# One product in each up quarter of a feed-forward made as two narrower ones, at widths that change from quarter to quarter

## The chip, the cores and the metric

The kernel runs on one core of one Trainium2 chip. The metric is the device time of one execution in microseconds (us). A smaller number is better. The time before is the median of 3 runs.

## What is computed

Two transformer blocks, one after the other, on 256 tokens of 1024 features in fp32. The part that the change touches is the feed-forward of the first block:

```
h = rmsnorm(x, ffn_norm[i])
u = causal_dwconv(h @ w_up[i], conv_w[i], conv_b[i])
x = x + (jax.nn.gelu(u) * (h @ w_gate[i])) @ w_down[i]
```

`w_up` and `w_gate` are 1024 x 2816, `w_down` is 2816 x 1024. Ahead of it stand the attention and the retention of the first block, behind it a gated embedding, and then the second block: a delta rule, sparse attention and a mixture of 16 experts.

## The kernel before

Every fp32 product is made as three products of the type fp32r. A weight matrix `w` is split into a high part `w_hi` and a rest `w_lo`, and so are the activations (`h_hi`, `h_lo`); the sum of high x high, high x low and low x high is added up in one place of PSUM. The function `three` issues these three. In the up projections `weight_stationary` is true: a 128 x 128 piece of the weights is the stationary operand, and 256 columns of `h`, one for each token, are the moving operand. Its passes are `((0, 0), (0, 1), (1, 0))`: pass 0 is `w_hi` with `h_hi`, pass 1 is `w_hi` again with `h_lo`, pass 2 is `w_lo` with `h_hi`. In a row of the profile the moving operand is named first (`h_lo,w_hi`).

The weights come as a stream of quarters of 128 x 1024, which pass through a ring of six slots (`raw`, `w_hi`, `w_lo`). SyncE issues the loads, ScalarE copies the high part (L635), GpSimd subtracts for the low part (L594, two instructions of 128 x 512 for a quarter), and TensorE waits for `lo_done` at the head of each quarter.

`feature_quarter` multiplies one quarter: a loop over 8 values of `k`, and `three` in each, so 24 products of 256 columns that all add into the same half bank (`dst`, 128 x 256). `up_block` makes four such quarters: two of `w_up` and then two of `w_gate`. `ffn_step` makes two up blocks and a down block of four quarters with 512 moving columns (`row_quarter`, 12 products in each). The step is written out once as the start, then runs four times in a loop (`Fori(1, FFN_STEPS)`, with `FFN_STEPS` = 5), and a last up block stands behind the loop, followed by the products of the gated embedding (`p_hi`, `p_lo`) and the last down products. In the start, the first two quarters are made by `first_quarters`, which does not call `feature_quarter`; `spread_root` puts in a small product of its own.

The order of TensorE's work is the order in which the program writes it.

Once the first two quarters of an up block are there, VectorE scales them (L2334), ScalarE and VectorE do the convolution (L763, L2342), ScalarE applies the gelu (L775), VectorE multiplies by the gate (L2348, L2351), and the result is split again for the down products (ScalarE L780, VectorE L2354).

Of the kernel before, what the change touches and what calls it, by code (L numbers as in the profile page):

```python
# [29 lines left out]
S = 256  # L30
NT = S // P
D = 1024
KD = D // P
# [24 lines left out]
B_FFN_LAST = B_FFN + 3 * FFN_STEPS  # L58
# [255 lines left out]
def program(nc, weights, smalls, x_in, p_in, vec_in, rows, con_in, slot_in, sel_in, pos_in, out):  # L314

    ctx = ExitStack()
    with ctx:
        made = {}

        def sem(name):  # L320

            if name not in made:
                made[name] = ctx.enter_context(nc.semaphore(name))
            return made[name]

        def sb(name, cols, dt=F32):
            return ctx.enter_context(nc.sbuf_tensor(name, [P, cols], dt))
# [7 lines left out]
        h_hi = sb("h_hi", KD * S, F32R)  # L335
        h_lo = sb("h_lo", KD * S, F32R)
# [8 lines left out]
        h_hi, h_lo, g_hi, g_lo = (x[:, :].rearrange("p (k s) -> p k s", s=S) for x in (h_hi, h_lo, g_hi, g_lo))  # L345
# [47 lines left out]
        bias = bias.rearrange("p (h s) -> p h s", s=S)  # L393

        (conv, act, ple, _, norm_row) = carve(1536, 2 * 512, 2 * 512, NT * D, NT * 512, D)
        conv = conv.rearrange("p (b f s) -> p b f s", b=2, s=S)
        act = act.rearrange("p (b n) -> p b n", b=2)
# [39 lines left out]
        for of, at, name in ((g_upper, 0, "g_upper_first"), (g_tri, 4 * PLE_CHUNKS * S, "g_tri_first")):  # L437
# [3 lines left out]
        (o_squares,) = carve(ATTENTION, 1024)  # L441

        (_, _, _, _, e_act, selectors, comb, comb_t, route, slot_con, slot_route, logit_rows) = carve(0, TILES * D, TILES * D, NT * SLOTS, TILES * S, 1024, DENSE * P, NT * N_EXPERTS, S, 354, SLOT_CON_N,
                          200, S)

# [86 lines left out]
        def pair(u):  # L532

            return bank[2 * (u % 2)], bank[2 * (u % 2) + 1]
# [621 lines left out]
        def _(pe):  # L1156
            mm = nc.tensor.matmul

            def three(dst, w, h, start, stop, weight_stationary):

                passes = ((0, 0), (0, 1), (1, 0)) if weight_stationary else ((0, 0), (1, 0), (0, 1))
                for n, (i, j) in enumerate(passes):
                    a, b = (w[i], h[j]) if weight_stationary else (h[j], w[i])
                    ins = mm(dst, a, b, start=start and n == 0, stop=stop and n == 2, skip_group_check=True)  # L1164
                return ins

            def quarter(q):
                return w_hi[:, ring(q)], w_lo[:, ring(q)]

            def await_quarter(n):  # L1170

                pe.wait_ge(sem("lo_done"), n + 1)
# [7 lines left out]

                pe.wait_ge(sem(f"pair_free{u % 2}"), 2 * (u // 2) + 2)

            def feature_quarter(n, q, dst, h=(h_hi, h_lo), norm=None, middle=None):


                if isinstance(n, int) and n == 0:
                    pe.wait_ge(sem("first_low_half"), 1)
                else:
                    await_quarter(n)
                w = [x.rearrange("p (k c) -> p k c", c=P) for x in quarter(q)]  # L1190
                for k in range(KD):
                    if isinstance(n, int) and n == 0 and k == KD // 2:
                        await_quarter(n)
                    if middle and k == KD // 2:
                        middle()
                    if norm is not None:

                        pe.wait_ge(sem("h_lo_done"), KD * norm + k + 1)
                    ins = three(dst, [x[:, k, :] for x in w], [x[:, k, :] for x in h], k == 0, k == KD - 1, True)
                ins.then_inc(sem("quarter_done"), 1)  # L1200

            def feature_project(b, u, beside=lambda f: None, norm=None, middle=lambda f: None, bank_free=lambda i: None):
# [30 lines left out]
            def token_half(q, u, f, t):  # L1233

                if t == 0:
                    await_quarter(q)
                w = [x.rearrange("p (k c) -> p k c", c=512) for x in quarter(q)]
                for j in range(2):
                    k = 2 * f + j
                    ins = three(pair(u)[t][:, :], [x[:, j, :] for x in w],  # L1240
                                [x[:, k, t * P:(t + 1) * P] for x in (h_hi, h_lo)], k == 0, k == KD - 1, False)
                if t:
                    ins.then_inc(sem("quarter_done"), 1)
                return ins
# [22 lines left out]
            def spread_root(n, to):  # L1267

                i = ROOT_ROWS.index(n)
                pe.wait_ge(sem("root_widened"), NT * i + NT)  # L1270
                for t in range(NT):
                    ins = mm(bank[to][:, t * P:(t + 1) * P], root_wide[:, t, :], ident, start=True, stop=True)
                ins.then_inc(sem("root_spread"), 1)
# [163 lines left out]
            def first_quarters(q0, norm, of):  # L1437

                dst = [of[:, f * S:(f + 1) * S] for f in range(2)]
                await_quarter(q0)  # L1440
                half_quarter(q0, q0, dst[0], range(4), norm)
                await_read(8)
                turn_half(norm, 1)
                await_quarter(q0 + 1)
                half_quarter(q0 + 1, q0 + 1, dst[1], range(4), norm, first_of_bank=False)
                for f in range(2):
                    half_quarter(q0 + f, q0 + f, dst[f], range(4, KD), norm).then_inc(sem("quarter_done"), 1)

            def up_block(base, q0, i, free, norm=None):

                pe.wait_ge(sem(f"pair_free{1 - i}"), free)
                if norm is not None:
                    first_quarters(base + q0, norm, pair(1 - i)[0])
                for f in range(0 if norm is None else 2, 4):
                    if norm is not None and f == 3:
                        spread_root(norm, 4)
                    feature_quarter(base + q0 + f, q0 + f, pair(1 - i)[f // 2][:, f % 2 * S:(f % 2 + 1) * S])

            def down_block(base, q0, n_up, start, stop, count=4):
                for k in range(count):  # L1460
                    if k % 2 == 0:

                        pe.wait_ge(sem("act_lo_done"), n_up + k // 2 + 1)
                    row_quarter(base + q0 + k, q0 + k, bank[4:8], (g_hi, g_lo), k, start and k == 0,
                                stop and k == count - 1)


            def ffn_step(base, n, start):
                up_block(base, 0, 0, n + 8, 1 if start else None)
                up_block(base, 4, 1, n + 10)  # L1470
                if start:
                    pe.wait_ge(sem("root_row_ready"), 2)
                down_block(base, 8, n, start, False)

            ffn_step(4 * B_FFN, 0, True)
            with pe.Fori(1, FFN_STEPS) as i:
                ffn_step(i * 12 + 4 * B_FFN, i * 2, False)
            n = 2 * FFN_STEPS
            up_block(4 * B_FFN_LAST, 0, 0, n + 8)

            pe.wait_ge(sem("pair_free0"), n + 10)
            pe.wait_ge(sem("p_split"), 2)
            q = 4 * B_PLE_DOWN
            for t in range(NT):
                if t == 1:
                    pe.wait_ge(sem("act_lo_done"), n + 1)
                for k in range(2):
                    await_quarter(q + k)
                    for c in range(2):
                        ins = three(bank[2 * t + c][:, :], [x[:, c * 512:(c + 1) * 512] for x in quarter(q + k)],  # L1490
                                    [x[:, k, t * P:(t + 1) * P] for x in (p_hi, p_lo)], k == 0, k == 1, False)
# [3 lines left out]
            for c in range(2):  # L1495
                for k in range(2):
                    await_quarter(q + 2 + k)
                    for t in range(NT):
                        ins = three(bank[4 + 2 * t + c][:, :], [x[:, c * 512:(c + 1) * 512] for x in quarter(q + 2 + k)],
                                    [x[:, k, t * P:(t + 1) * P] for x in (g_hi, g_lo)], False, k == 1, False)  # L1500
# [16 lines left out]
            for t in range(NT):  # L1517
                for f in range(4):
                    ins = token_half(4 * (B_PLE_GATE + 1) + f, 23, f, t)
# [324 lines left out]
            for i in range(2):  # L1844
                for f in range(4):
                    q = 4 * (B_PROJ + i) + f
# [10 lines left out]
                    w = [x.rearrange("p (f k c) -> p f k c", f=2, c=P) for x in quarter(q)]  # L1857
                    for j in range(2):
                        if j:
                            delta_slot(2 * (q - 4 * B_IQ) + 1, delta_step)  # L1860
                        for k in range(4):
                            ins = three(pair(u)[f % 2][:, j * S:(j + 1) * S], [x[:, j, k, :] for x in w],
                                        [x[:, 4 * (1 - i) + k, :] for x in (g_hi, g_lo)], k == 0, k == 3, True)
# [85 lines left out]
            for t in range(NT):  # L1949
                ins = nc.tensor.transpose(bank[3][0:N_EXPERTS, t * P:(t + 1) * P], comb[:, t, :], ident)  # L1950
# [4 lines left out]
            for e in range(DENSE):  # L1955
                ins = mm(bank[2][:, e * S:(e + 1) * S], selectors[0:N_EXPERTS, e * P:(e + 1) * P], comb_t, start=True, stop=True)
# [21 lines left out]
            for k in range(4):  # L1978
                if k % 2 == 0:
                    pe.wait_ge(sem("expert_lo_done"), k // 2 + 1)  # L1980
                q = 4 * (B_MOE + 2) + k
# [10 lines left out]
            def y_banks(tile):  # L1992
                return bank[4 + 2 * (tile % 2)], bank[5 + 2 * (tile % 2)]
# [74 lines left out]
            for c in range(2):  # L2068
                for k in range(2):
                    ins = three(y_banks(GROUPS)[c][:, :], [x[:, c * 512:(c + 1) * 512] for x in quarter(N_QUARTERS + last + k)],  # L2070
                                [x[:, k, 0:P] for x in (g_hi, g_lo)], False, k == 1, False)
# [1052 lines left out]
```

## Time and profile before

| | |
|---|---|
| median of 3 runs | 842.63 us (842.61 to 843.84) |
| the profiled execution's own time | 846.45 us |
| its span, first to last instruction | 844.6 us |
| mean granted TensorE clock | 0.991 |
| TensorE matmul busy | 823.0 us, 97% |
| TensorE weight load busy | 737.5 us, 87% |
| VectorE, ScalarE, GpSimd busy | 59%, 55%, 56% |

A matmul record's end is modelled, and records of neighbours overlap. So what tells how fast TensorE goes is the distance from one start to the next, not the duration in a record. PE rows are the matmuls, PEld rows the loads of the stationary operand. Every matmul record has a weight-load record of its own (6271 of each).

### The profile page before, as it was taken

What the parts mean: (1) busy time and instruction counts of PE and PEld (TensorE: products, weight loads), DVE (VectorE), ACT (ScalarE), POOL (GpSimd) and SP (SyncE); (2) the same over time, 40 slices, a digit from 0 to 9 for tenths busy, and PEclk for the clock granted to TensorE, in tenths of its full rate; (3) what the DMA queues carried; (4) which work ended last, traced back from release to release, by engine and by line L of the source; (5) the groups of instructions that cost most, each with busy time, mean ns of one, the idle gap of its engine ahead of it and who ended that gap; (6) DMA issues with size and microseconds to landing.
All of it is one profiled execution on the core that took longest, in us unless ns stands there. A gap on an engine that the chain in (4) does not pass through costs nothing.

```text
span 844.6 us, 16277 instructions
## 1 busy us (share of the span) xinstructions
PE 823.0 (97%) x6271; PEld 737.5 (87%) x6271; DVE 496.5 (59%) x1000; ACT 466.3 (55%) x735; POOL 476.0 (56%) x372
## 2 busy tenths in 40 slices
PE   9899999999999999899999999999999999999995
PEld 7899889999999997689988999999889888888883
DVE  3832444682422315663497835347478699999983
ACT  5423654735644466764448433235456578878763
POOL 5997476989999898686854443366868000000000
PEclk9999999999999999999999999999999999999998
DMA  8654144545655554444642213232545689999931
GB/s 315 226 200 177 74 150 175 175 176 199 204 193 199 199 199 150 150 151 150 218 151 100 101 52 102 101 103 100 197 150 177 273 335 370 352 392 340 393 108 50
DMA packets 24141, 160.98 MB, mean 191 GB/s; under 512 B 3200, under 2 KB 3728, under 8 KB 5392
## 3 DMA queue, kind: packets, MB, share of 16 engines
q1 hardware_dynamic: 21456, 154.67, 50.1%
q10 hardware_dynamic: 2624, 5.44, 1.9%
q8 instruction: 44, 0.72, 0.3%
q14 instruction: 17, 0.14, 0.0%
HBM read 157.62 MB, written 1.05 MB: 188 GB/s over the span
## 4 chain that ended last, share of the span: by engine, by line
PE 86%; DVE 7%; ACT 3%; DMA 2%; issue 1%; ACTq 0%; SPq 0%; DVEq 0%
PE bank L1164 72%; PE bank L1713 3%; PE bank L1930 1%; DVE work L2220 1%; DMA row<-dt_bias_dram 1%; PE bank L2047 1%; DMA raw<-weights_dram 1%; DVE work L2529 1%; ACT w_hi L635 1%; PE bank L1262 1%; DVE bank L2589 1%; PE bank L1325 1%; PE bank L1311 1%; DVE best L2588 0%; PE bank L1742 0%
## 5 line engine op out<-in xcount | busy, mean ns | idle before, releaser
L594 POOL TENSOR_TENSOR w_lo<-raw,w_hi 128x512 fp32r<-128x512 f32 x368 | 475.8, 1328 | 175.2 <-ACT w_hi L635 175.1
L1164 PE MATMUL bank<-h_hi,w_hi 128*128 128x256 f32 x864 | 247.4, 286 | 0.5 <-POOL w_lo L594 0.5
L1164 PE MATMUL bank<-h_lo,w_hi 128*128 128x256 f32 x864 | 241.6, 280 | 0.0
L1164 PE MATMUL bank<-h_hi,w_lo 128*128 128x256 f32 x864 | 241.5, 280 | 0.0
L635 ACT ACTIVATE w_hi<-raw 128x1024 fp32r<-128x1024 f32 x184 | 187.9, 1058 | 82.4 <-PE bank L1164 51.2
L1164 PEld LDWEIGHTS bank<-h_hi,w_hi 128*128 128x128 f32 x864 | 162.6, 188 | 4.9 <-POOL w_lo L594 1.4
L1164 PEld LDWEIGHTS bank<-h_hi,w_lo 128*128 128x128 f32 x864 | 163.9, 190 | 0.0
L1164 PEld LDWEIGHTS bank<-h_lo,w_hi 128*128 128x128 f32 x864 | 162.7, 188 | 0.3
L1164 PE MATMUL bank<-w_hi,g_hi 128*128 128x512 f32 x208 | 81.6, 392 | 0.0
L1164 PE MATMUL bank<-w_hi,g_lo 128*128 128x512 f32 x208 | 81.0, 390 | 0.0
L1164 PE MATMUL bank<-w_lo,g_hi 128*128 128x512 f32 x208 | 81.0, 389 | 0.0
L3007 DVE TENSOR_TENSOR w_lo<-raw,w_hi 128x1024 fp32r<-128x1024 f32 x54 | 63.0, 1218 | 5.8 <-ACT w_hi L644 5.6
L1164 PE MATMUL bank<-w_hi,slot_hi 128*128 128x512 f32 x144 | 57.7, 401 | 0.0
L644 ACT ACTIVATE w_hi<-raw 128x1024 fp32r<-128x1024 f32 x54 | 53.6, 1058 | 7.0 <-PE bank L1164 7.0
L1164 PE MATMUL bank<-w_hi,h_hi 128*128 128x512 f32 x128 | 52.6, 411 | 4.0 <-DVE work L2155 2.4
L1164 PE MATMUL bank<-w_hi,slot_lo 128*128 128x512 f32 x144 | 56.3, 391 | 0.0
L1164 PE MATMUL bank<-w_lo,slot_hi 128*128 128x512 f32 x144 | 56.2, 390 | 0.0
L1164 PE MATMUL bank<-w_hi,h_lo 128*128 128x512 f32 x128 | 51.5, 402 | 0.0
L1164 PE MATMUL bank<-w_lo,h_hi 128*128 128x512 f32 x128 | 51.3, 401 | 0.0
L2334 DVE TENSOR_TENSOR bank<-bank,work 128x512 f32<-128x512 f32 x11 | 7.7, 697 | 67.4 <-PE bank L1164 67.4
L1164 PEld LDWEIGHTS bank<-w_hi,g_lo 128*128 128x128 f32 x208 | 39.0, 188 | 8.2
L1164 PEld LDWEIGHTS bank<-w_hi,g_hi 128*128 128x128 f32 x208 | 39.1, 188 | 8.1 <-issue 0.4
(408 smaller groups left out, 1353.9 us busy)
## 6 DMA issues: line engine op xcount, KB each, us to landing
raw<-weights_dram SPq DMA_DIRECT2D x119, 1024.0 KB, 4.8
spare<-weights_dram SPq DMA_DIRECT2D x18, 1024.0 KB, 6.1
tok<-weights_dram SPq DMA_DIRECT2D x9, 1024.0 KB, 5.7
x_sb<-x_dram SPq DMA_DIRECT2D x2, 512.0 KB, 4.6
work<-final_norm_dram ACTq DMA_DIRECT2D x2, 512.0 KB, 5.4
work<-work ACTq DMA_DIRECT2D x8, 128.0 KB, 4.8
work<-constants_dram ACTq DMA_DIRECT2D x1, 640.0 KB, 5.1
con<-constants_dram ACTq DMA_DIRECT2D x1, 520.0 KB, 3.8
```

The source lines that it names most:

```text
L594: ins = nc.gpsimd.tensor_tensor(w_lo[:, part], raw[:, part], w_hi[:, part].bitcast(F32), ALU.subtract)
L635: nc.scalar.activation(w_hi[:, ring(q)], raw[:, ring(q)], ACT.Copy).then_inc(sem("hi_done"), 1)
L644: nc.scalar.activation(w_hi[:, ring(n)], slot_quarter(i), ACT.Copy).then_inc(sem("slot_hi_done"), 1)
L1164: ins = mm(dst, a, b, start=start and n == 0, stop=stop and n == 2, skip_group_check=True)
L1262: ins = nc.tensor.transpose(bank[turned_bank(n, k)][:, k % 2 * S + t * P:k % 2 * S + (t + 1) * P], x3[:, t, k * P:(k + 1) * P], ident)
L1311: ins = mm(bank[4 + odd][:, t * P:t * P + (t + 1) * P], q3[own, f, t * P:(t + 1) * P], k3[own, kf(f), 0:(t + 1) * P], start=True, stop=True)
L1325: ins = nc.tensor.transpose(bank[6 + n % 2][:, i * P:(i + 1) * P], p[:, i * P:(i + 1) * P], ident)
L1713: ins = mm(bank[b][rows, column + m * w:column + (m + 1) * w], lhs[rows, m, :], rhs[rows, m, :], start=True, stop=True)
L1930: ins = mm(dst, x[t][:, k * P:(k + 1) * P], one_hot[:, t, of], start=t == 0 and x is tok_hi, stop=t == 1 and x is tok_lo, skip_group_check ...
L2047: ins = mm(total[t, c][:, :], one_hot_t[:, tile, t * P:(t + 1) * P], y[:, tile, c * 512:(c + 1) * 512], start=tile == 0 and y is y_hi, sto ...
L2220: V.tensor_scalar(bias[:, h, :], dist, -(HD ** 0.5) * 2.0 ** (-8.0 * (h + 1) / HEADS), None, ALU.mult).then_inc(sem("bias_ready"), 1)
L3007: V.tensor_tensor(w_lo[:, ring(n)], slot_quarter(i), w_hi[:, ring(n)].bitcast(F32), ALU.subtract)\
```

## The change

`three` gets an argument `cut`, a width and a pass. In that pass the product is issued twice, over the moving columns 0 to width and width to 256, with the same stationary operand and the two parts of the same PSUM region. `feature_quarter` hands it on at `k == 1` alone, so that one product in 24 becomes two. The widths are those of `FFN_CUTS`, by the number of the quarter in the step. The pass is 1 in the start, 0 in the loop and 2 in the last block.

```diff
+            FFN_CUTS = (128, 64, 192, 32, 96, 160, 224, 128)
 
-            def three(dst, w, h, start, stop, weight_stationary):
+            def three(dst, w, h, start, stop, weight_stationary, cut=None):
...
                     a, b = (w[i], h[j]) if weight_stationary else (h[j], w[i])
-                    ins = mm(dst, a, b, start=start and n == 0, stop=stop and n == 2, skip_group_check=True)
+                    if cut and n == cut[1]:
+                        columns = slice(0, cut[0]), slice(cut[0], S)
+                        for c in columns:
+                            ins = mm(dst[:, c], a, b[:, c], start=False, stop=False, skip_group_check=True)
+                    else:
+                        ins = mm(dst, a, b, start=start and n == 0, stop=stop and n == 2, skip_group_check=True)
                 return ins
...
-                    ins = three(dst, [x[:, k, :] for x in w], [x[:, k, :] for x in h], k == 0, k == KD - 1, True)
+                    ins = three(dst, [x[:, k, :] for x in w], [x[:, k, :] for x in h], k == 0, k == KD - 1, True,
+                                cut if k == 1 else None)
...
-                    feature_quarter(base + q0 + f, q0 + f, pair(1 - i)[f // 2][:, f % 2 * S:(f % 2 + 1) * S])
+                    feature_quarter(base + q0 + f, q0 + f, pair(1 - i)[f // 2][:, f % 2 * S:(f % 2 + 1) * S],
+                                    cut=(FFN_CUTS[q0 + f], cut_pass))
...
-                up_block(base, 0, 0, n + 8, 1 if start else None)
-                up_block(base, 4, 1, n + 10)
+                up_block(base, 0, 0, n + 8, 1 if start else None, cut_pass=1 if start else 0)
+                up_block(base, 4, 1, n + 10, cut_pass=1 if start else 0)
...
-            up_block(4 * B_FFN_LAST, 0, 0, n + 8)
+            up_block(4 * B_FFN_LAST, 0, 0, n + 8, cut_pass=2)
```

On TensorE, in the first quarter of the loop's body, the rows before are these (bank2 is the region of PSUM that this quarter adds into, 128x256 the moving columns):

```order
L1164 MATMUL bank2<-h_hi,w_hi 128x256
L1164 MATMUL bank2<-h_lo,w_hi 128x256
L1164 MATMUL bank2<-h_hi,w_lo 128x256
L1164 MATMUL bank2<-h_hi,w_hi 128x256
L1164 MATMUL bank2<-h_lo,w_hi 128x256
```

and in the changed kernel, at the same place (L1171 is the uncut product, L1169 a part of the cut one):

```order
L1171 MATMUL bank2<-h_hi,w_hi 128x256
L1171 MATMUL bank2<-h_lo,w_hi 128x256
L1171 MATMUL bank2<-h_hi,w_lo 128x256
L1169 MATMUL bank2<-h_hi,w_hi 128x128 x2
L1171 MATMUL bank2<-h_lo,w_hi 128x256
```

The fourth product has become two of 128 columns; nothing else moved.

In the fourth quarter of the last block, with pass 2 and the width 32, TensorE's rows of the changed kernel are these:

```order
L1171 MATMUL bank3<-h_hi,w_hi 128x256
L1171 MATMUL bank3<-h_lo,w_hi 128x256
L1169 MATMUL bank3<-h_hi,w_lo 128x32
L1169 MATMUL bank3<-h_hi,w_lo 128x224
L1171 MATMUL bank3<-h_hi,w_hi 128x256
```

Here the third product of `k == 1` is made as 32 and 224 columns. In the program text 18 quarters are changed like this (6 in the start, 8 in the loop's body, 4 in the last block), and no other engine's rows differ in anything but line numbers.

## Rows read from the trace of the kernel before

**Rows 1.** The page, part 2: tenths in 40 slices, PE and its granted clock.

```profile
PE   9899999999999999899999999999999999999995
PEclk9999999999999999999999999999999999999998
```

**Rows 2.** The page, part 4: the chain that ended last, by engine.

```profile
PE 86%; DVE 7%; ACT 3%; DMA 2%; issue 1%; ACTq 0%; SPq 0%; DVEq 0%
```

**Rows 3.** The chain in order of time: start, us, what.

```profile
146.64 164.66 PE bank L1164 x1176
```

**Rows 4.** The chain between 311 and 327 us.

```profile
311.32 0.71 DVE bank L2334
...
318.99 0.70 DVE g_lo L2354
...
319.74 7.10 PE bank L1164 x30
```

**Rows 5.** Stretches: PE busy, count, PEclk, DMA share, GB/s.

```profile
146.64:311.30 164.66, 164.66 (x1178) 1.00 0.54 191
```

**Rows 6.** Groups of PE between 146.64 and 311.3 us.

```profile
L1164 PE MATMUL bank<-h_hi,w_hi 128*128 128x256 f32 x313 | 88.0, 281 | 0.0
...
L1164 PE MATMUL bank<-w_hi,g_hi 128*128 128x512 f32 x80 | 31.1, 389 | 0.0
```

**Rows 7.** The page, part 5: costliest groups.

```profile
L594 POOL TENSOR_TENSOR w_lo<-raw,w_hi 128x512 fp32r<-128x512 f32 x368 | 475.8, 1328 | 175.2 <-ACT w_hi L635 175.1
...
L1164 PEld LDWEIGHTS bank<-h_hi,w_hi 128*128 128x128 f32 x864 | 162.6, 188 | 4.9 <-POOL w_lo L594 1.4
...
L1164 PEld LDWEIGHTS bank<-h_lo,w_hi 128*128 128x128 f32 x864 | 162.7, 188 | 0.3
```

**Rows 8.** Timeline of PE from 149.78 us: start, duration.

```profile
149.78 0.28 PE L1164 MATMUL bank<-h_lo,w_hi 128*128 128x256 f32 x1
...
152.96 0.28 PE L1164 MATMUL bank<-h_lo,w_hi 128*128 128x256 f32 x1
```

**Rows 9.** Timeline of PEld at the same place.

```profile
149.90 0.19 PEld L1164 LDWEIGHTS bank<-h_hi,w_hi 128*128 128x128 f32 x1
150.02 0.19 PEld L1164 LDWEIGHTS bank<-h_lo,w_hi 128*128 128x128 f32 x1
```

**Rows 10.** Timeline of PE, a run of 512-column products.

```profile
122.11 0.39 PE L1164 MATMUL bank<-w_hi,g_lo 128*128 128x512 f32 x1
...
125.97 0.39 PE L1164 MATMUL bank<-w_lo,g_hi 128*128 128x512 f32 x1
```

**Rows 11.** Timeline of PE: sixteen 128-column fp32r products between 512-column ones.

```profile
657.71 0.39 PE L1164 MATMUL bank<-w_hi,g_lo 128*128 128x512 f32 x1
657.94 0.22 PE L1930 MATMUL bank<-one_hot,g_hi 128*128 128x128 f32 x1
658.00 0.28 PE L1930 MATMUL bank<-one_hot,tok_lo 128*128 128x128 f32 x1
...
659.97 0.40 PE L1164 MATMUL bank<-w_lo,g_hi 128*128 128x512 f32 x1
```

**Rows 12.** Timeline of PE: sixteen 2-column products between 256-column ones.

```profile
456.54 0.28 PE L1164 MATMUL bank<-h_hi,w_lo 128*128 128x256 f32 x1
456.65 1.84 PE L1651 MATMUL bank<-con,work 128*128 128x2 f32 x16
...
458.67 0.28 PE L1164 MATMUL bank<-h_hi,w_lo 128*128 128x256 f32 x1
```

**Rows 13.** Timeline of PE, behind the last up block.

```profile
319.26 0.39 PE L1164 MATMUL bank<-w_hi,p_lo 128*128 128x512 f32 x1
319.74 0.50 PE L1164 MATMUL bank<-w_hi,p_hi 128*128 128x512 f32 x1
```

**Rows 14.** Waits of the weight load: us, times, longest.

```profile
PEld bank L1164 <- POOL w_lo L594: 1.4, 3, 0.7
```

**Rows 15.** Stretches: PE, PEld, DVE, ACT, POOL busy, PEclk, DMA share, GB/s.

```profile
358.40:361.90 3.50, 3.50 (x11) 2.69 (x10) 3.39 (x10) 3.29 (x7) 2.20 (x2) 0.51 0.00 0
```

More of the change, by code:

```diff
@@ L1181, in await_read, with feature_quarter @@
                 pe.wait_ge(sem(f"pair_free{u % 2}"), 2 * (u // 2) + 2)
-            def feature_quarter(n, q, dst, h=(h_hi, h_lo), norm=None, middle=None):
+            def feature_quarter(n, q, dst, h=(h_hi, h_lo), norm=None, middle=None, cut=None):
                 if isinstance(n, int) and n == 0:
@@ L1447, in first_quarters, with up_block @@
                     half_quarter(q0 + f, q0 + f, dst[f], range(4, KD), norm).then_inc(sem("quarter_done"), 1)
-            def up_block(base, q0, i, free, norm=None):
+            def up_block(base, q0, i, free, norm=None, cut_pass=0):
                 pe.wait_ge(sem(f"pair_free{1 - i}"), free)
```

## The prediction

> **What bounds the kernel now.** I read the page first. TensorE is busy in every slice and its granted clock is full nearly everywhere [rows 1], and the chain that ended last is 86% PE [rows 2]. So TensorE's own pace is the time, if the busy share can be believed; records of matmuls overlap, and a short stall could hide under them. The chain in order of time answers that for the place of the change: from 146.64 us on it is one piece of 164.66 us of TensorE's products [rows 3]. In that stretch the clock is at 1.00, which is the 2.4 GHz level [rows 5].
>
> The second check is a count. The timeline gives the pace of 256-column products: 27 intervals between 149.78 and 152.96 us, 3.18 / 27 = 0.118 us from start to start [rows 8]. For 512 columns it is 17 intervals between 122.11 and 125.97 us, 3.86 / 17 = 0.227 us [rows 10]. Between 146.64 and 311.3 us the trace has 313 + 313 + 312 = 938 products of 256 columns and 3 x 80 = 240 of 512 (the three passes, of which one row each stands there) [rows 6]. 938 x 0.1178 + 240 x 0.2271 = 110.5 + 54.5 = 165.0 us against 164.66 us of span [rows 5]. There is no room for a stall: through the whole feed-forward TensorE goes product after product, and what is put in there is paid in full. GpSimd keeps up: two instructions of 1.328 us make the low part of a quarter, 2.66 us [rows 7], while TensorE takes 24 x 0.118 = 2.83 us for an up quarter and 12 x 0.227 = 2.72 us for a down quarter. A slower TensorE only gives it more room.
>
> **How many cuts.** The start has 6 quarters that go through `feature_quarter` (two in its first block, since `first_quarters` makes the others, and four in its second), the loop 8 in each of 4 turns, the last block 4: 6 + 32 + 4 = 42. Each adds one matmul and one weight load, and leaves the number of moving columns as it was. Nothing is removed and nothing changes place; no wait and no DMA is added. The semaphore increment stays on the last product of a quarter, and `k == 1` carries none.
>
> **What one more product costs.** The columns are the same, so all of the cost is what comes with an instruction. The stationary operand is loaded for every product, even where it is the same as that of the product before: the passes `h_hi,w_hi` and `h_lo,w_hi` share their `w_hi` piece, stand next to each other, and each has its 864 loads of 188 ns [rows 7]. These loads overlap: one starts 0.12 us behind the other, in step with the matmuls [rows 8, 9]. So the question is how close two loads can follow each other where the matmuls are too short to hold them apart.
>
> Two places of the trace show it. Sixteen products of 2 columns with a full 128 x 128 stationary operand stand between 256-column products: from 456.54 to 458.67 us are 2.13 us, which hold these sixteen and three intervals of 256-column products (at 0.118 us 0.35 us); (2.13 - 0.35) / 16 = 0.111 us each [rows 12]. Two columns take nearly no time to stream, so this is the pace of the loads alone. Sixteen fp32r products of 128 columns stand between 512-column ones: from 657.71 to 659.97 us are 2.26 us, with two 512-column intervals of 0.227 us in them; (2.26 - 0.454) / 16 = 0.113 us each [rows 11]. So a product of 2 columns and one of 128 cost the same, 0.112 us, and 256 columns cost 0.118 us. The floor is the weight load, and up to a width near 256 the columns are hidden under it.
>
> It follows that a cut costs the same at every width: both parts (32 to 224 columns) sit under the floor, and 0.118 us become 2 x 0.112 = 0.224 us, 0.106 us more. The two estimates of the floor give 0.104 and 0.108; if each part kept the pace of a 256-column product it would be 0.118. No row shows a part of 160, 192 or 224 columns; they lie between 128 (0.113) and 256 (0.118), which bounds them at the same 0.118. I take 0.106, the middle of the two estimates, since every cut has a part of 128 columns or fewer, and 224 is the widest of the others.
>
> The Trainium skill (TensorE: Matmul & The Clock Gate, section LDWEIGHTS (loading the stationary operand)) gives a load the time of its columns at 1.2 GHz, by which 128 columns would be 107 ns. By that, as an estimate, a cut would cost 2 x 0.107 - 0.118 = 0.096 us and 40 of them 3.8 us; the trace, at 0.111 to 0.113 us, comes close, and I go by the trace.
>
> **Where it is paid, and where not.** The cuts in the last block's third and fourth quarter have cover. Its first two quarters are done at about 311.3 us, and from there the chain leaves TensorE: it goes through VectorE's scaling, the gelu and the split of the product, and comes back to TensorE at 319.74 us [rows 4]. TensorE meanwhile makes the two gate quarters and the products of the embedding, and then it has a hole: the product that starts at 319.26 us would be followed at 319.26 + 0.23 = 319.49 us, and the next one starts at 319.74 us [rows 13]. That is 0.25 us of room for two cuts of 0.106 = 0.21 us. They fit, and 40 cuts are left: 40 x 0.106 = 4.24 us. Had that cover gone, it would be 4.45 us.
>
> Behind the feed-forward everything hangs on its result, so the delay is carried to the end. What could take some back is that GpSimd gets ahead of TensorE during the slower stretch: all waits of the weight load for it in the whole kernel are 1.4 us in 3 places [rows 14], and TensorE may be waited for by others at these places. I count nothing for it.
>
> **The sum.** The profiled execution of before has a span of 844.6 us and a time of its own of 846.45 us; I expect 848.9 and 850.7 us. The median of the runs without a profile is 842.63 us, 3.8 us lower than the profiled one. 842.63 + 4.24 = 846.9 us, 0.5% slower.
>
> **One source of scatter.** In one stretch of 3.5 us behind the feed-forward the granted clock is 0.51, which is the 1.2 GHz level, while products are running [rows 15]. At full clock the same products would take about 1.8 us, so such a dip costs 1.7 us. Whether it falls on busy products may vary with where the stretch lies in time; the change shifts it by 4 us. I allow 1.7 us below for a dip that is missed, and above it 1.2 us, the spread of the three runs shown. A time within 0.2% (1.7 us) of before is about what a measurement of this kernel can't tell from no change.
>
> **The rivals.**
> *The second part needs no load.* If the hardware or the build left out a load whose operand is already in the array, a cut would cost only what two products cost more than one of their width together: 2 x 0.118 - 0.227 = 0.009 us, by the pace at 256 and 512 columns [rows 8, 10]. 40 of them are 0.4 us, 843.0 us, no change. It decides if the extra per cut is under 1.7 / 40 = 0.04 us. Against it speak the 864 loads of `h_lo,w_hi` [rows 7]. Chance 4%.
>
> *A load is ready ahead of time.* The first 128-column product behind a 512-column one is followed 0.06 us later, not 0.11 (657.94, 658.00) [rows 11]: its successor's weights seem to have been there. If a lone cut always found its weights ready like that, one of its two parts would cost 0.06 us, and a cut 0.06 + 0.112 - 0.118 = 0.054 us, 2.2 us in all, 844.8 us. Against it: the sum over the whole run of sixteen comes to 0.113 each, so the early start is given back at the run's end, and a 256-column product leaves its load only 0.006 us of slack. Chance 8%. The Trainium skill (same page, section Back-to-back issue gap) gives products of 128 columns a sustained pace of about 81 ns each; by it a cut would be 2 x 0.081 - 0.118 = 0.044 us, 1.8 us in all and 844.4 us. The trace has 0.113 us at 128 columns and 0.227 us at 512, where that section has 131 ns, so this case does not bear it out.
>
> *A part costs more than the floor.* A narrow product right behind a wide one, a part that starts inside a bank's half, or widths such as 96 and 224 could have a price that no row shows. If the extra load stood bare, it would be its 0.188 us [rows 7], 42 x 0.188 = 7.9 us and 850.5 us. Chance 6%.
>
> *The delay is taken back behind the feed-forward*, by the clock dip that falls elsewhere (1.7 us) together with the waits for GpSimd (up to 1.4 us): 842.63 + 4.24 - 3.1 = 843.8 us, no change that can be told. Nothing shows that the two come together. Chance 3%.
>
> **How the numbers follow.** My forecast has 79%. Its own range is from 40 x 0.104 = 4.2 us less the dip of 1.7 us, 845.1 us, to 42 x 0.118 = 5.0 us plus 1.2 us, 848.8 us; these are the ends I give, and the load that is ready and the cases of no change lie below them, the bare load above, 21% in all. Slower by over 0.2% (above 844.3 us) are the forecast, the bare load, and the ready load in part: 0.79 + 0.06 + 0.05 = 0.90. Within 0.2% are the case without a load (0.04), most of the delay taken back (0.02 of 0.03), and the rest of the ready load (0.03): 0.09. Faster is left 0.01, for a delay that is more than taken back: no part of the change removes work.
>
> **What the profile after should show.** 6271 + 42 = 6313 records of each kind (less what is missing). The cut products in two groups of parts with a load of 188 ns to each. In the loop, from the start of the product ahead of a cut to the start of the second product behind it, 0.118 x 3 + 0.106 = 0.46 us where before there were 0.35, at all widths alike; the place of the gap inside will move with the width. A turn of the loop longer by 8 x 0.106 = 0.85 us. The hole at 319.5 us nearly closed. I am wrong if the gap differs by width, if the second part has no load, or if the stretch from 137 to 320 us grows by 4.2 us and the span does not.

## The result, and the profile after

The changed kernel takes 843.69 us (median of 22 runs, 842.42 to 849.7) against 842.41 us (median of 22 runs, 841.69 to 858.5) before: a ratio of 1.0020, 95% interval 1.0013 to 1.0027. One run of before, at 858.5 us, counts as slow and is not in the ratio. The changed kernel is 1.1 to 2.3 us slower, where 4.2 us were forecast; the time lies below the stated range.

The page of the changed kernel, part 1, shows the 42 products more that were counted, and no more busy time for them (822.0 us, where it was 823.0):

```profile
PE 822.0 (98%) x6313; PEld 736.9 (88%) x6313; DVE 492.8 (59%) x1000; ACT 466.2 (55%) x735; POOL 475.4 (57%) x372
```

The groups of the changed kernel by form show the cut products and their loads. The other forms of L1169 look the same; all 84 parts have a load of 188 ns of their own, in three groups of 64, 12 and 8:

```profile
L1169 PE MATMUL bank<-h_hi,w_hi 128*128 128x128 f32 x16 | 2.7, 248 | 0.0
...
L1169 PE MATMUL bank<-h_hi,w_hi 128*128 128x32 f32 x8 | 1.5, 184 | 0.0
...
L1169 PEld LDWEIGHTS bank<-h_hi,w_hi 128*128 128x128 f32 x64 | 9.7, 188 | 0.0
```

To compare the feed-forward alone, I measure a turn of the loop, from the first 256-column product behind a down block to the same one a turn later. In the timeline of PE of the kernel before:

```profile
171.49 0.28 PE L1164 MATMUL bank<-h_hi,w_hi 128*128 128x256 f32 x1
...
204.99 0.28 PE L1164 MATMUL bank<-h_hi,w_hi 128*128 128x256 f32 x1
```

and of the changed one:

```profile
167.04 0.28 PE L1171 MATMUL bank<-h_hi,w_hi 128*128 128x256 f32 x1
...
200.71 0.28 PE L1171 MATMUL bank<-h_hi,w_hi 128*128 128x256 f32 x1
```

33.50 us have become 33.67 us (to the nanosecond 33.493 and 33.660): 0.17 us for eight cuts, where 0.85 were forecast. The reason stands in the products that were not changed. The timeline of PE of the changed kernel, around a cut of width 64:

```profile
170.12 0.28 PE L1171 MATMUL bank<-h_hi,w_lo 128*128 128x256 f32 x1
170.24 0.36 PE L1169 MATMUL bank<-h_hi,w_hi 128*128 128x64 f32 x2
170.44 0.31 PE L1171 MATMUL bank<-h_lo,w_hi 128*128 128x256 f32 x1
170.58 0.28 PE L1171 MATMUL bank<-h_hi,w_lo 128*128 128x256 f32 x1
...
170.81 0.28 PE L1171 MATMUL bank<-h_lo,w_hi 128*128 128x256 f32 x1
...
172.97 0.28 PE L1171 MATMUL bank<-h_hi,w_lo 128*128 128x256 f32 x1
```

The gap at the cut came out as forecast: from the product ahead of it (170.12 us) to the second product behind it (170.58 us) are 0.46 us, where three uncut intervals took 0.35. But from 170.81 to 172.97 us are 19 intervals of uncut 256-column products: 2.16 / 19 = 0.114 us. Before, the same products stood 0.118 us apart [rows 8]. The stretches say it with counts. A stretch of 20 us of up quarters in the kernel before, and one in the changed kernel:

```profile
206.00:226.00 20.00, 20.00 (x172) 1.00 0.60 210
```

```profile
168.00:188.00 20.00, 20.00 (x179) 1.00 0.46 163
```

In the second, seven cuts have made seven records more; 179 - 7 = 172, the same amount of work in the same time. What the cuts cost, the faster products gave back. The granted clock is 1.00 in both.

The products `con,x_sb` belong to the norms and mark the ends of the feed-forward. From the second group of eight of them ahead of it to the first one behind it are 137.70 to 326.86 us before and 133.19 to 323.14 us after: 189.16 and 189.95 us, 0.8 us more for the feed-forward. From there to the last instruction are 517.8 and 517.7 us, so nothing was taken back behind it.

### The profile page after: what moved, and what is told of

Read it like the earlier page. It is cut to its first block, busy times and chain, and to the rows that moved or that the text cites. A ratio compares the mean times of both kernels' runs of the same rounds, so it can differ in the third digit from the quotient of the medians.

```text
span 840.9 us, 16361 instructions
## 1 busy us (share of the span) xinstructions
PE 822.0 (98%) x6313; PEld 736.9 (88%) x6313; DVE 492.8 (59%) x1000; ACT 466.2 (55%) x735; POOL 475.4 (57%) x372
## 4 chain that ended last, share of the span: by engine, by line
PE 89%; DVE 6%; ACT 2%; DMA 1%; issue 1%; POOL 1%; SPq 0%; DVEq 0%; ACTq 0%
PE bank L1171 74%; PE bank L1722 3%; PE bank L1939 1%; PE bank L2056 1%; PE bank L1169 1%; DMA raw<-weights_dram 1%; DVE work L2538 1%; PE bank L1270 1%; DVE bank L2598 1%; POOL w_lo L594 1%; PE bank L1333 1%; PE bank L1319 1%; DVE best L2597 0%; PE bank L1751 0%; PE bank L1810 0%
## 5 line engine op out<-in xcount | busy, mean ns | idle before, releaser
L1171 PE MATMUL bank<-h_lo,w_hi 128*128 128x256 f32 x858 | 240.1, 280 | 0.0
L1171 PE MATMUL bank<-h_hi,w_lo 128*128 128x256 f32 x860 | 239.2, 278 | 0.0
L1171 PE MATMUL bank<-h_hi,w_hi 128*128 128x256 f32 x832 | 236.9, 285 | 0.3 <-POOL w_lo L594 0.3
L1171 PEld LDWEIGHTS bank<-h_lo,w_hi 128*128 128x128 f32 x858 | 161.6, 188 | 0.4
L1171 PEld LDWEIGHTS bank<-h_hi,w_lo 128*128 128x128 f32 x860 | 161.9, 188 | 0.0
L1171 PEld LDWEIGHTS bank<-h_hi,w_hi 128*128 128x128 f32 x832 | 156.6, 188 | 4.3 <-issue 1.7
L1171 PE MATMUL bank<-w_hi,g_hi 128*128 128x512 f32 x208 | 81.7, 393 | 0.0
L1171 PE MATMUL bank<-w_hi,g_lo 128*128 128x512 f32 x208 | 81.0, 390 | 0.0
L1171 PE MATMUL bank<-w_lo,g_hi 128*128 128x512 f32 x208 | 81.0, 389 | 0.0
L1171 PE MATMUL bank<-w_hi,slot_hi 128*128 128x512 f32 x144 | 57.7, 401 | 0.0
L1171 PE MATMUL bank<-w_hi,slot_lo 128*128 128x512 f32 x144 | 56.3, 391 | 0.0
L1171 PE MATMUL bank<-w_lo,slot_hi 128*128 128x512 f32 x144 | 56.2, 390 | 0.0
L1171 PE MATMUL bank<-w_hi,h_hi 128*128 128x512 f32 x128 | 51.3, 401 | 1.0 <-DVE h_lo L2182 0.7
L1171 PE MATMUL bank<-w_hi,h_lo 128*128 128x512 f32 x128 | 50.6, 395 | 0.0
L1171 PE MATMUL bank<-w_lo,h_hi 128*128 128x512 f32 x128 | 50.5, 394 | 0.0
L1171 PEld LDWEIGHTS bank<-w_hi,g_lo 128*128 128x128 f32 x208 | 39.0, 188 | 8.2
L1171 PEld LDWEIGHTS bank<-w_hi,g_hi 128*128 128x128 f32 x208 | 39.1, 188 | 8.1 <-issue 0.4
```

## The experiments

Each kernel is compared with the kernel before on the same chip; the kernels themselves ran on several chips, so they are compared with each other by their ratios and by the turns of the loop.

**The theories.** A: 256-column products have two paces, 0.1178 and 0.1134 us. A cut has the price that was forecast, but it also brings the fast pace for the products behind it. B: a cut is cheap by itself, some 0.02 to 0.04 us, since its load is ready ahead of time, as in the rival of the prediction.

### One cut for each run of up quarters

```diff
-                                    cut=(FFN_CUTS[q0 + f], cut_pass))
+                                    cut=(128, cut_pass) if q0 == 0 and f == (0 if norm is None else 2) else None)
```

> One cut per run of up quarters (width 128, first quarter through feature_quarter in the start, in each turn of the loop and in the last block: 6 cuts in place of 42). Theory A, two paces: a cut costs about 0.12 us and puts all 256-column products behind it at 0.1134 us instead of 0.1178 until the next 512-column run. Then a turn of the loop goes from 33.49 us before to 33.49 + 0.12 - 188 x 0.0044 = 32.78 us, and the whole to about 3.5 us less than before (ratio 0.996). Theory B, a cut is cheap by itself because its load is ready ahead (0.02 to 0.04 us) and the pace plays no part: a turn of 33.51 to 33.53 us, the whole as before within 0.3 us.

840.66 us, ratio 0.9972 (0.9962 to 0.9983): faster than before. The timeline of PE of this kernel, at a turn's cut, at the end of its up quarters' first stretch, and at the heads of two turns:

```profile
168.64 0.28 PE L1171 MATMUL bank<-h_hi,w_lo 128*128 128x256 f32 x1
168.76 0.33 PE L1169 MATMUL bank<-h_hi,w_hi 128*128 128x128 f32 x2
168.93 0.33 PE L1171 MATMUL bank<-h_lo,w_hi 128*128 128x256 f32 x1
169.10 0.28 PE L1171 MATMUL bank<-h_hi,w_lo 128*128 128x256 f32 x1
...
184.75 0.28 PE L1171 MATMUL bank<-h_hi,w_lo 128*128 128x256 f32 x1
...
201.35 0.28 PE L1171 MATMUL bank<-h_hi,w_hi 128*128 128x256 f32 x1
...
234.14 0.28 PE L1171 MATMUL bank<-h_hi,w_hi 128*128 128x256 f32 x1
```

From 169.10 to 184.75 us are 138 products: 15.65 / 138 = 0.1134 us each, all behind a single cut. A turn is 234.14 - 201.35 = 32.79 us, where A said 32.78 and B 33.51 or more. A stretch of 20 us holds 179 products, none of them cut, against 172 of before:

```profile
203.00:223.00 20.00, 20.00 (x179) 1.00 0.60 210
```

The whole gained 1.4 to 3.2 us and not 3.5. In the start, the four narrow products of `spread_root` (from 142.93 us) come behind the cut. Ahead of them the pace is 0.113 us, and the 119 products behind them go at 0.118 us again, which costs 0.5 us of the forecast: a break can also end the fast pace. The first turn of the loop has a short wait at 184.91 us.

### The same cut at width 224

```diff
-                                    cut=(FFN_CUTS[q0 + f], cut_pass))
+                                    cut=(224, cut_pass) if q0 == 0 and f == (0 if norm is None else 2) else None)
```

> Six cuts as in the kernel with one cut per run, but at width 224 and not 128. In the kernel with all cuts at 224 the first cut of a turn, made in the slow pace, was followed by slow products, and only the second cut brought the fast pace. Theory A (two paces, the switch is what pays): this cut leaves the pace at 0.1178, and the bare price of a cut is seen, 0.104 us: a turn of 33.493 + 0.104 = 33.60 us, the whole 0.6 us above before. A rival: one cut of any width brings the fast pace for the rest of the run: a turn of 32.8 us and 3 us less than before.

843.47 us, ratio 1.0018 (1.0001 to 1.0036). The timeline of PE at the same places:

```profile
168.67 0.29 PE L1169 MATMUL bank<-h_hi,w_hi 128*128 128x224 f32 x2
168.81 0.36 PE L1171 MATMUL bank<-h_lo,w_hi 128*128 128x256 f32 x1
169.01 0.28 PE L1171 MATMUL bank<-h_hi,w_lo 128*128 128x256 f32 x1
169.13 0.28 PE L1171 MATMUL bank<-h_hi,w_hi 128*128 128x256 f32 x1
...
185.50 0.28 PE L1171 MATMUL bank<-h_lo,w_hi 128*128 128x256 f32 x1
...
201.94 0.28 PE L1171 MATMUL bank<-h_hi,w_hi 128*128 128x256 f32 x1
```

This is the price of a cut with no change of pace behind it. The cut product and the one behind it take 169.01 - 168.67 = 0.34 us where two uncut ones take 0.236, so 0.104 us more; the forecast had 0.106. And the pace stays slow: 169.13 to 185.50 us are 139 intervals of 0.1178 us. A turn (168.32 to 201.94 us) is 33.62 us, and the whole grew by 0.1 to 3.0 us, where 0.6 were expected. Between this kernel and the one above nothing differs but where the one product is cut, 224 or 128 columns, and a turn differs by 0.83 us.

It would be wrong to read from this that 224 columns never bring the fast pace. The cut of the last block has the same width in the same trace; it stands at the same `k`, in the pass `h_hi,w_lo` and not `h_hi,w_hi`:

```profile
303.39 0.29 PE L1169 MATMUL bank<-h_hi,w_lo 128*128 128x224 f32 x2
...
303.97 0.28 PE L1171 MATMUL bank<-h_hi,w_hi 128*128 128x256 f32 x1
...
304.99 0.28 PE L1171 MATMUL bank<-h_hi,w_hi 128*128 128x256 f32 x1
```

Ahead of it the products stand 0.118 us apart. From 303.97 to 304.99 us are 9 intervals of 0.113 us, and the pace stays there.

### The cut late in the run

```diff
-                                cut if k == 1 else None)
+                                cut if k == 6 else None)
...
+                                    cut=(128, cut_pass) if q0 == 0 and f == (2 if norm is None else 3) else None)
```

> Six cuts of width 128, moved late in the run: at k = 6 of the third quarter of each first up block (fourth in the start). Theory A: the products ahead of the cut keep 0.1178 us, those behind it go at 0.1134; in a turn 125 products are behind it: 33.493 + 0.12 - 125 x 0.0044 = 33.06 us, the whole about 2.2 us below before. Rival (the fast pace comes from something else in the changed program, such as where its code lies): a turn as in the kernel with the early cut, 32.79 us, or as before, 33.49 us, with no change of pace at the cut.

840.96 us, ratio 0.9980 (0.9970 to 0.9990). The timeline of PE in a turn:

```profile
201.47 0.28 PE L1171 MATMUL bank<-h_hi,w_hi 128*128 128x256 f32 x1
...
209.12 0.28 PE L1171 MATMUL bank<-h_hi,w_lo 128*128 128x256 f32 x1
209.24 0.33 PE L1169 MATMUL bank<-h_hi,w_hi 128*128 128x128 f32 x2
...
209.58 0.28 PE L1171 MATMUL bank<-h_hi,w_lo 128*128 128x256 f32 x1
...
210.49 0.28 PE L1171 MATMUL bank<-h_lo,w_hi 128*128 128x256 f32 x1
...
234.53 0.28 PE L1171 MATMUL bank<-h_hi,w_hi 128*128 128x256 f32 x1
```

The 65 intervals ahead of the cut (201.47 to 209.12 us) are 0.1177 us each, the 8 behind it (209.58 to 210.49 us) 0.114. The change of pace has moved with the cut, and a cause elsewhere in the program is out. The turn is 33.06 us, as A said; the whole gained 0.8 to 2.5 us, where 2.2 were expected.

### Twice as many cuts

```diff
-                                cut if k == 1 else None)
+                                cut if k in (1, 4) else None)
```

> The cuts of the change, made at k = 1 and again at k = 4 of each quarter (84 cuts). Theory A: the second cut finds the fast pace already there and pays its full 0.11 to 0.12 us: a turn goes from 33.66 us in the changed kernel to about 34.6 us, the whole 4.7 us above the changed kernel, 6 us above before (ratio 1.007). Theory B: each more cut costs what the first did net, 0.02 us: a turn of 33.83 us, 0.9 us above the changed kernel.

848.64 us, ratio 1.0092 (1.0056 to 1.0128). The heads of two turns in the timeline of PE:

```profile
168.81 0.28 PE L1171 MATMUL bank<-h_hi,w_hi 128*128 128x256 f32 x1
...
203.47 0.28 PE L1171 MATMUL bank<-h_hi,w_hi 128*128 128x256 f32 x1
```

A turn takes 34.66 us against 33.66 with one cut a quarter: 1.00 / 8 = 0.125 us for each cut that finds the fast pace already there. That is more than the 0.104 us in the slow pace, since it is counted from 0.1134 us and not from 0.1178. B's 33.83 us is out.

### All cuts at width 224

```diff
-            FFN_CUTS = (128, 64, 192, 32, 96, 160, 224, 128)
+            FFN_CUTS = (224,) * 8
```

> All 42 cuts at width 224 (224 + 32 columns). Theory A: in the changed kernel eight intervals around a cut of 224 sum to 0.907 us against 0.916 to 0.930 at the other widths, because no slow products follow it; a turn of 33.58 to 33.60 us against 33.66, the whole 0.3 to 0.4 us below the changed kernel. Theory B, all widths alike: 33.66 us.

844.36 us, ratio 1.0017 (1.0008 to 1.0026), as the changed kernel. A turn is 33.69 us and not the 33.58 to 33.60 that I expected. The timeline of PE, behind the first cut of a turn and around the second:

```profile
169.53 0.28 PE L1171 MATMUL bank<-h_hi,w_lo 128*128 128x256 f32 x1
...
172.12 0.29 PE L1169 MATMUL bank<-h_hi,w_hi 128*128 128x224 f32 x2
...
173.05 0.28 PE L1171 MATMUL bank<-h_lo,w_hi 128*128 128x256 f32 x1
...
174.86 0.28 PE L1171 MATMUL bank<-h_hi,w_lo 128*128 128x256 f32 x1
```

The first cut leaves the pace slow (169.53 to 172.12 us are 22 intervals of 0.118 us), and the second, of the same width and in the same pass, brings the fast one (173.05 to 174.86 us are 16 intervals of 0.113 us). So it is in all four turns. The width alone doesn't decide whether a cut in the slow pace takes. The run with one cut at 224 came from this. Behind a cut of 224 made in the fast pace, that pace is there again at once.

### Two 256-column products at the end of the down block

```diff
             def row_quarter(n, q, banks, h, k, start, stop, bank_free=None, cut=None):
...
-                                    [x[:, k, t * P:(t + 1) * P] for x in h], start, stop, False)
+                                    [x[:, k, t * P:(t + 1) * P] for x in h], start, stop, False,
+                                    cut if (t, c) == (NT - 1, 1) else None)
...
-                                stop and k == count - 1)
+                                stop and k == count - 1, cut=(256, 2) if k == count - 1 else None)
```

with no cut in the up quarters.

> No cut in the up quarters; instead the last 512-column product of each down block is made as 256 + 256. Its own price is 2 x 0.118 - 0.227 = 0.009 us. If the fast pace only needs some break in the rhythm ahead of the run of 256-column products, a turn is 33.49 + 0.01 - 192 x 0.0044 = 32.66 us and the whole about 3.5 us below before; if it needs a product that is shorter than the weight load (theory A in its narrow form), a turn stays at 33.50 us. Theory B: 33.50 us.

840.34 us, ratio 0.9972 (0.9961 to 0.9982). The timeline of PE at the head of a turn:

```profile
233.63 0.40 PE L1169 MATMUL bank<-w_hi,g_lo 128*128 128x256 f32 x2
233.86 0.29 PE L1171 MATMUL bank<-h_hi,w_hi 128*128 128x256 f32 x1
233.98 0.28 PE L1171 MATMUL bank<-h_lo,w_hi 128*128 128x256 f32 x1
...
234.56 0.28 PE L1171 MATMUL bank<-h_hi,w_hi 128*128 128x256 f32 x1
234.67 0.28 PE L1171 MATMUL bank<-h_lo,w_hi 128*128 128x256 f32 x1
```

The pair takes 0.23 us like the 512-column product that it replaces, and a few products later the fast pace is there. A turn (201.18 to 233.86 us) is 32.68 us, where 32.66 was expected. So the switch doesn't need a product that is shorter than the weight load: the narrow form of A fell here. A break in the rhythm just ahead of the run was enough. The whole gained 2.1 us (1.5 to 3.3) and not 3.5. The feed-forward alone, by the same marks as above, is 3.3 us shorter in the trace, and its first turn has a short wait for GpSimd's low part (0.2 us of the weight load).

### Other widths, in the loop alone

```diff
+                                    cut=(32, 0) if q0 == 0 and f == 0 and cut_pass == 0 else None)
```

and the same with 192.

> One cut a turn, in the loop alone, of width 32 (narrow part first, then 224). 128 + 128 at this place brought the fast pace, 224 + 32 did not. If the switch needs the second part's start pushed far from where the slow pace has it, a narrow first part may do it as well: a turn of 33.493 + 0.12 to 0.14 - 188 x 0.0044 = 32.80 us. If a pair of 32 and 224 never does it, whichever comes first, a turn is 33.62 us, as with 224 + 32.

> One cut a turn, in the loop alone, of width 192 (then 64). The switch works at 128 and not at 224: if 192 is on the side of 128, a turn is 32.79 us, if on that of 224, 33.62 us. No theory here says which.

One run each, so without an interval: 840.07 and 839.83 us, beside 842.76 us before on the same chip. Turns of 32.80 us (200.48 to 233.28) and 32.79 us, alike in all whole turns behind the first. So at this one place, the first quarter of a turn in the slow pace, 32 + 224, 128 + 128 and 192 + 64 bring the fast pace and 224 + 32 does not.

### Fast pace everywhere

To the kernel with 256 + 256, one cut of 128 + 128 is added in each other long slow run:

```diff
+            CUT_QUARTERS = (4 * B_RQ + 1, 4 * B_MQ + 2, 4 * B_IQ + 1, 4 * B_KV + 1)
...
+                                    middle=lambda: middle(f), cut=(128, 1) if q in CUT_QUARTERS else None)
...
+                                    cut=(128, 1) if norm is not None and f == 3 else None)
...
+                                        cut=(128, 1) if i == 0 and f in (1, 3) and j == 0 and k == 1 else None)
...
+                                    cut=(128, 1) if i == 0 and f == 3 else None)
```

> The kernel with 256 + 256 at the end of each down block, and besides one cut of 128 + 128 in each other long run of 256-column products that the traces show in the slow pace: the start's last quarter of its first block, two in the projections ahead of the feed-forward, two in the second block's projections, two in the output projections, one in the dense experts. Theory A: each costs about 0.12 us and turns 60 to 160 products from 0.1178 to 0.1134 us (in the output projections from 0.1199): about 2.5 us below the kernel with 256 + 256 alone, some 838 us in all. If the second cut kind doesn't bring the fast pace there, it is 1 us above that kernel instead.

838.95 us, ratio 0.9957 (0.9944 to 0.9969). By the medians it gained 1.4 us on the kernel with 256 + 256, and not 2.5, and the intervals of the two ratios overlap. In the output projections the pace stayed at 0.120 us (timeline of PE: 577.02 to 577.98 us are 8 intervals of 0.12), so those two cuts cost without giving. And TensorE outruns GpSimd in the loop's first turn, by more than in the kernel with 256 + 256:

```profile
182.54 0.28 PE L1171 MATMUL bank<-h_hi,w_lo 128*128 128x256 f32 x1
183.23 0.38 PE L1171 MATMUL bank<-h_hi,w_hi 128*128 128x256 f32 x1 [0.42 <-POOL w_lo L594]
183.45 0.28 PE L1171 MATMUL bank<-h_lo,w_hi 128*128 128x256 f32 x1
```

Behind this wait the products go at 0.118 us to the end of the turn's up quarters, so a wait can end the fast pace too. This turn takes 33.61 us, where it took 32.95 in the kernel with 256 + 256. An up quarter at the fast pace is 24 x 0.1134 = 2.72 us, and GpSimd needs 2.66 us for its low part [rows 7]: the next bound is close.

The last kernel leaves out the cut in the index projection (`4 * B_IQ + 1`) and the two in the output projections:

> The kernel with cuts in all runs, without the cuts that brought nothing there (one in the index projection, two in the output projections, whose pace stayed at 0.120 us). Theory A: those three cost 0.1 to 0.13 us each and gave back almost nothing, so the whole is 0.3 us below that kernel, about 838.6 us; a turn stays at 32.68 us.

839.05 us, ratio 0.9951 (0.9938 to 0.9965), the lowest ratio of all, though its interval overlaps with that of the kernel with all the cuts: the 0.3 us expected can't be told. A turn is 32.68 us, as expected. Both kernels beat the kernel before and the changed one.

## Why the prediction was wrong

**What was right.** The bound: TensorE without a gap, every cut in it paid. The count, 42, and a load for every part: 6313 records, 84 loads of 188 ns. The gap at a cut, 0.46 us, and the price of a cut: forecast 0.106 us from the floor of the weight load, measured 0.104 us where the pace doesn't change. The rival without a second load is out, and so is the load that is ready ahead of time. Its sum (844.8 us) lies nearer to the result than mine, but for a wrong reason: the kernel with twice the cuts, at 0.125 us for each more, refutes it. The rival in which the delay is taken back behind the feed-forward is out as well, since that part took 517.8 us before and 517.7 after. That the result is so near to no change is a coincidence of two sizes, as the next part shows.

**The step that failed** is the sentence that a cut "leaves the number of moving columns as it was. Nothing is removed and nothing changes place", and with it the sum, which took 0.118 us for every product that isn't cut, before and after. What the runs showed in its place: the 0.118 us are one of two paces, and a cut can move the products behind it to the other. Counted from the slow pace, eight cuts in a turn of the loop cost 8 x 0.104 to 0.107 = 0.83 to 0.86 us, and the turn grew by 0.17, so some 0.68 us came back, at 0.0044 us each from about 155 of the 192 products. The run with one cut and the run with the late cut show that the cut is the cause, and those at 128 and 224 that it is not the program's length or the number of cuts. The prediction's own sign, a feed-forward longer by 4.2 us, failed with it: 0.8 us.

**The trace of before had shown it.** The estimate of the load's floor used the stretch around 456.54 us [rows 12], and just ahead of it the same kind of product goes at the fast pace (timeline of PE of the kernel before):

```profile
455.52 0.28 PE L1164 MATMUL bank<-h_hi,w_lo 128*128 128x256 f32 x1
...
456.42 0.28 PE L1164 MATMUL bank<-h_lo,w_hi 128*128 128x256 f32 x1
```

8 intervals in 0.90 us are 0.113 us, and behind the sixteen narrow products it is 0.118 again. I took the pace from one stretch [rows 8], saw that it filled the feed-forward, and did not ask why the same products went faster elsewhere. With that question, a rival would have stood in the prediction in which a cut of 0.106 us and 23 products a quarter at 0.0044 us less (0.10 us) nearly cancel, at 843 us.

**The cover of the last block's two cuts** was there, but smaller in its use: the hole behind 315.62 us is 0.40 us from start to start, 0.18 us beyond a product's 0.227, where 0.25 was before [rows 13] and 0.04 was expected. Part of that is that the quarters that fill it had become faster too.

**What stays open.** The feed-forward grew by 0.8 us in the two traces, and the medians differ by 1.28 us (the ratio says 1.1 to 2.3 us). The rest is not explained, and single traces are too coarse for it. Among the kernels with the same code there, the part ahead of the feed-forward takes 133.2 to 134.9 us and the part behind it 517.5 to 519.0 us. The trace of before stands out with 137.70 us ahead: TensorE has a wait of 2.4 us there for VectorE (L2155), followed by 3.4 us at a granted clock of 0.50, which is the 1.2 GHz level. The prediction added up 850.7 us from that execution; with the change it was 842.67 us, since 4.5 us are missing ahead of the feed-forward and 3.4 of the forecast 4.2 in it.

Nor do the runs say why there are two paces, or what decides whether a break changes them. 224 + 32 columns in the slow pace did nothing as a turn's first cut, and took as its second cut and in the last block. `spread_root` ended the fast pace in the kernel with one cut; in the kernel of before it stood in the slow pace and changed nothing. "A break in the rhythm" is a name for what these places share, not a cause that was shown.

## What to carry to other kernels

Take the pace of a repeated instruction from several stretches of the trace, by starts and counts, and when the same instruction has two paces, ask of every edit which of them it leaves behind, before its own cost is summed. In this kernel, bound by a dense stream of fp32r products of 256 columns, a single break at the head of each run (the last 512-column product made as 256 + 256, which costs under 0.01 us by the starts) was worth 2.1 us of 842, and breaks in every quarter cost more than they gave. Whether a break takes is to be read from the starts behind it, at each place anew: a cut at 224 + 32 columns at the head of a turn, or one at 128 + 128 in the output projections, cost and gave nothing, and a break or a wait behind the first can end the fast pace again.

## What the runs showed of the hardware

- fp32r products of 256 columns with a 128 x 128 stationary operand run at 0.1134 or at 0.1178 us from start to start, both at a granted clock of 1.00. Either pace holds on for over a hundred products (138 in one row of starts above at the fast one, 139 at the slow one). In the output projections they stand 0.120 us apart, in the kernel before too, also at a granted clock of 1.00.
- In the loop, the pace was slow at the head of the up quarters behind every run that ends in 512-column products, in every turn, also where it had been fast ahead of it. As a turn's first break, 32 + 224, 128 + 128, 192 + 64 or, at the end of the 512-column run, 256 + 256 switched it to fast, and 224 + 32 did not. As a turn's second cut, and in the last block in another pass, 224 + 32 did.
- The fast pace can be ended as well as started: by the four narrow products of `spread_root` (0.113 us ahead of them, 0.118 behind), by a wait of some 0.6 us for `w_lo` (once; one of some 0.3 us in the kernel with 256 + 256 left the pace fast), and in the kernel before by sixteen products of 2 columns.
- The same code can stand at either pace in two traces. In the projections ahead, which the change doesn't touch, a stretch from 18 to 26 us holds 73 products in the trace of the kernel before and 70 in that of the kernel with the late cut, which is as before up to there:

```profile
18.00:26.00 8.00, 8.00 (x73) 1.00 0.69 258
```

```profile
18.00:26.00 8.00, 8.00 (x70) 1.00 0.73 269
```

  Over the some 160 products of that run it is, as an estimate, 0.7 us. Two executions of one kernel may differ by as much; no two traces of the same kernel are on record to show it.
- Every product has a weight load of its own in the records, also when the operand is the one already there (84 loads for the 84 parts). Rows of narrow products keep 0.111 us (2 columns) and 0.113 us (128 columns) on average [rows 11, 12], and a cut at 32 + 224 and one at 224 + 32 cost the same within 0.01 us: the cut product and the one behind it take 0.35 and 0.34 us.
